# Fourier mixing with half of the cosines and sines: one stage of a two-network kernel, and where its instructions move

## The chip, the core and the metric

The program runs on one NeuronCore of a Trainium2 chip. The core has five engines with queues of their own that run side by side and wait for each other through semaphores: TensorE (PE, matrix products into PSUM), VectorE (DVE), ScalarE (ACT), GpSimd (POOL) and SyncE (SP, which issues most of the DMA transfers). The metric is the device time of one launch in microseconds (us); the kernel before takes 2376.23 us (median of three runs, 2372.3 to 2379.91).

## The reference

Two small networks run one after the other on 256 tokens of 1024 features, in float32. The last layer of the second network mixes its tokens by a Fourier transform instead of attention:

```python
def fourier_mix(h):
    b, l, d = h.shape
    hg = h.reshape(b, l, FNET_GROUPS, d // FNET_GROUPS).astype(F32)
    f = jnp.fft.fft2(hg, axes=(1, 3), norm="ortho").real
    return f.reshape(b, l, d).astype(h.dtype)
...
            y = fourier_mix(h) @ w_f
        x = x + g1 * rms_norm_2(y, norm_g[i, 1])
        h = modulate_2(rms_norm_2(x, norm_g[i, 2]), sh2, sc2)
        x = x + g2 * rms_norm_2(conv_ffn(h, ffn_w_up[i], ffn_conv_w[i], ffn_conv_b[i], ffn_w_down[i]), norm_g[i, 3])
```

With FNET_GROUPS = 4 and d = 1024, each of four groups is a block of 256 tokens by 256 features h, of which the real part of the two-dimensional transform is wanted. With C and S the 256 by 256 matrices of cosines and sines (divided by 16 here), the real part is C h C - S h S. Each row of C is symmetric about its middle (column 256-f equals column f) and each row of S antisymmetric, so that columns 0 to 128 of both determine the rest.

## The kernel before, in words

Everything is kept transposed: features lie on the 128 partitions and tokens along the free dimension, so a tile such as `hT` is eight chunks of 128 features by 256 tokens, two chunks to each Fourier group. The kernel is one straight program for each engine, written out by hand: `sp_program`, `pe_program`, `act_program`, `dve_program` and `pool_program` call small functions (`pe_fourier`, `dve_fourier`, ...) in the order in which the engine is to execute them, and each step waits for named counts of other engines. Nothing is reordered by a scheduler, so an instruction that waits holds up all that stands behind it on its engine.

PSUM banks 0 to 3 are given out in turn (`bank.turn`); a bank can be taken again when the instruction named in `bank.until` is done. Weights come in by DMA into ring slots of 1 MB. A matrix product with weights is made of three products of rounded halves (`mm3`): ACT copies a unit of 128x1024 weights to its high half (L386, `act_units`), and DVE or POOL subtracts that to get the low half (L392, `dve_units` and `pool_program`; the last argument of `sp_fm` says which of the two). Four buffers (HB) hold high halves, so at most four units are prepared ahead (`ahead`).

The Fourier stage of the last layer:

- The norm before it (tag `nA`) scales the eight chunks on DVE (L851) and shifts them on ACT (L816).
- `pe_fourier`, first step: for each group g and each half j of the tokens, two products of 128 tokens by 512 columns (256 cosines, 256 sines) into one bank, 16 products in all, begun when the norm is done with all eight chunks (`norm.done(7)`). DVE copies each bank to `fU` (L2767).
- Second step: for each group and each half i of the transformed features, four products of 128 by 256 that sum cosines with cosines and sines with negated sines, 32 in all. DVE copies each of the four banks to `fT` (L2770).
- ACT rounds each chunk to its high half (L867, `act_halves`), DVE forms the low half into `XL` (L872, `dve_halves`), and the output projection (`pe_out`, tag `out`) multiplies by `fourier_w_out`: 8 units of 24 products of 128x256.

Every matmul on float32 operands shows as two records in the trace, so 16 products are x32 there and 32 products x64; the products of rounded halves (fp32r, marked by an r at the tile's name) are one record each.

At the kernel's start there is one more place that matters here: `sp_mixer_first` loads the weights of the first projection ("qk", l, 0), whose low halves POOL forms, and `dve_program` runs the eight low halves of the first norm (`norm1[0].dve_low`, L858).

Of the kernel before, what the change touches and what calls it, by code (L numbers as in the profile page):

```python
# [16 lines left out]
T = 256  # L17
# [61 lines left out]
def dft_constants():  # L79
    n = np.arange(256)  # L80
    ang = 2.0 * np.pi * ((n[:, None] * n[None, :]) % 256) / 256.0
    cs = np.concatenate([np.cos(ang), np.sin(ang), -np.sin(ang)], axis=1) / 16.0
    return np.ascontiguousarray(cs.astype(np.float32))
# [140 lines left out]
def build(nc, A, out):  # L224
    CST_W = sum(w for _, w in CONST_COLS.values())
    with ExitStack() as ctx:
# [694 lines left out]
        def sp_mixer_first(sp, l):  # L921
            series()
            sp_fm(sp, ("qk", l, 0), A["w_in"][l], 0, "pool")
# [1633 lines left out]
        def act_out(act, l, hi, src, ready):  # L2557
            act_halves(act, ("out", l), hi, src, ready)
# [4 lines left out]
        def dve_out(dve, l, hi, src):  # L2563
            dve_halves(dve, ("out", l), hi, XL, src)
# [166 lines left out]
        fU = area(0)(4096)  # L2731
        fT = area(4096)(2048)
        fhi = area(6144)(2048, True)[1]

        def sp_fourier(sp):
            load(sp, ("dft",), by_rows(A["dft"]), 2, 768, MODS_IN)

        def pe_fourier(pe, norm):
            cs = chunk(("dft",), 2, 768)
            pe.wait_ge(*landed(("dft",)))  # L2740
            pe.wait_ge(*norm.done(7))
            for g in range(4):
                for j in range(2):
                    pe.wait_ge(*bank.turn("U", g, j))
                    for k in range(2):
                        t = mm(pe, bank["U", g, j][:, :], hT[:, (2 * g + k) * 256 + j * 128:(2 * g + k) * 256 + j * 128 + 128],
                               cs[:, k, 0:512], k == 0, k == 1)
                    t.then_inc(*pe_ffn.inc("U", g, j))
                    bank.until(("U", g, j), dve_ffn, "U", g, j)
            for g in range(4):  # L2750
                pe.wait_ge(*bank.turn("f", g))
# [7 lines left out]
                t.then_inc(*pe_ffn.inc("f", g))  # L2759
                bank.until(("f", g), dve_ffn, "f", g)  # L2760
            slots.until(("dft",), pe_ffn, "f", 3)
# [117 lines left out]
        def act_program(act):  # L2879
# [15 lines left out]
            act_out(act, 0, att.hi, att.oT, lambda k: dve_att["o", k])  # L2895
            for l in range(2):
                if l == 1:
                    normA[1].act(act)
                    act_units(act, ahead(("out", 1, 0, 0)))
                    act_out(act, 1, fhi, fT, lambda k: dve_ffn["f", k // 2])  # L2900
# [5 lines left out]
        def dve_program(dve):  # L2906
            dve_prologue(dve)
            for l in range(2):
                if l == 0:
# [5 lines left out]
                    for k in range(8):  # L2915
                        norm1[0].dve_low(dve, k)
# [8 lines left out]
            dve_out(dve, 0, att.hi, att.oT)  # L2925
            for l in range(2):
                if l == 1:
                    normA[1].dve(dve)
                    dve_units(dve, ahead(("out", 1, 0, 0)))
                    dve_fourier(dve)  # L2930
                    dve_out(dve, 1, fhi, fT)
# [86 lines left out]
```

## Time and profile before

| | |
|---|---|
| median of three runs | 2376.23 us (2372.3 to 2379.91) |
| profiled execution, its own time | 2380.68 us |
| its span in the trace | 2378.9 us |
| mean granted TensorE clock | 0.955 of full speed |
| PE busy | 2177.5 us (92%), 13659 records |
| DVE, ACT, POOL busy | 972.9, 671.7, 288.7 us |
| DMA | 657.92 MB, mean 277 GB/s |

The span is the time from the first to the last instruction of the profiled execution; 1.8 us lie outside it. A busy share is an average over stages with different limits, so the share of an engine says little on one stage; the chain of waits and the table of stretches say what the stage waits for. The granted clock has two levels, 2.4 GHz (1.00) and 1.2 GHz (0.50); a value between them is a mixture within the stretch. Busy times overlap: matmuls are pipelined, so the mean duration of one record is longer than the distance from one start to the next, and it is that distance (busy time over count) that adds up.

### The profile page before, as it was taken

The numbers are of one execution on the slowest core, as the hardware profiler recorded it, in microseconds if no ns is written. First come the engines' busy times: TensorE is split into PE (matmuls) and PEld (weight loads), VectorE is DVE, ScalarE is ACT, GpSimd is POOL, SyncE is SP. The second block draws the span as 40 slices with busy tenths as digits, with TensorE's granted clock in tenths as the row PEclk, the third lists the DMA queues.
The fourth block names the chain that finished last, engine by engine and source line by source line (L and its number), as shares of the span: only waits on it lengthen the run. The fifth ranks groups of instructions, "written<-read, shape, count | busy, mean of one in ns | idle before, by whom it ended". The sixth has DMA issues, their size and how long they took to land.

```text
span 2378.9 us, 31740 instructions
## 1 busy us (share of the span) xinstructions
PE 2177.5 (92%) x13659; PEld 1562.9 (66%) x13659; DVE 972.9 (41%) x1914; ACT 671.7 (28%) x1176; POOL 288.7 (12%) x147
## 2 busy tenths in 40 slices
PE   4998988999999999899899999999989899988998
PEld 3787674555555467777455555555756899968997
DVE  2465641111111146564221111111535677546776
ACT  2334421011111143443211011111123555424553
POOL 4543420000000034453000000000000000000000
PEclk7999989999999989999999999999999799887998
DMA  9865669999999976566899999996536365314550
GB/s 327 306 231 183 237 230 372 409 408 409 409 409 409 403 252 222 188 230 261 329 358 409 409 409 409 409 409 255 210 125 225 117 209 191 103 53 145 180 195 19
DMA packets 246844, 657.92 MB, mean 277 GB/s; under 512 B 12923, under 2 KB 124773, under 8 KB 234280
## 3 DMA queue, kind: packets, MB, share of 16 engines
q1 hardware_dynamic: 244032, 652.27, 72.6%
q8 instruction: 111, 1.82, 0.3%
q0 software_dynamic: 1184, 2.08, 0.3%
q10 hardware_dynamic: 1480, 1.45, 0.2%
q14 instruction: 37, 0.30, 0.0%
HBM read 654.70 MB, written 1.06 MB: 276 GB/s over the span
## 4 chain that ended last, share of the span: by engine, by line
PE 86%; DVE 9%; ACT 2%; SPq 1%; issue 1%; DMA 1%; ACTq 0%
PE ps L409 85%; DVE AR L1961 2%; SPq L341 1%; DVE AR L746 1%; DVE AR L2008 1%; DMA ring<-in_w_in 1%; DVE ARr L1636 0%; ACT HBr L386 0%; ACT AR L816 0%; PE ps L2462 0%; ACT AR L728 0%; DVE AR L2596 0%; DVE AR L1226 0%; DVE AR L1111 0%; DVE XLr L858 0%
## 5 line engine op out<-in xcount | busy, mean ns | idle before, releaser
L409 PE MATMUL ps<-ring,AR 128*64 128x512 f32 (+1 forms) x2016 | 522.9, 581 | 31.6 <-DVE AR L2008 31.6
L409 PE MATMUL ps<-XLr,HBr 128*128 128x256 f32 x1408 | 411.9, 293 | 44.8 <-DVE XLr L858 25.0
L409 PE MATMUL ps<-AR 128*128 128x128 f32 (+6 forms) x2088 | 380.8, 345 | 14.0 <-DVE AR L1942 7.5
L409 PEld LDWEIGHTS ps<-ring,AR 128*64 128x64 f32 (+1 forms) x2016 | 203.0, 141 | 271.4 <-issue 264.4
L392 POOL TENSOR_TENSOR ringr<-ring,HBr 128x1024 fp32r<-128x1024 f32 x112 | 270.9, 2434 | 803.2 <-ACT HBr L386 802.9
L409 PEld LDWEIGHTS ps<-AR 128*128 128x128 f32 (+2 forms) x2088 | 289.4, 191 | 119.8 <-issue 76.6
L409 PE MATMUL ps<-hTr,ringr 128*128 128x256 f32 x1280 | 367.4, 287 | 0.0
L409 PE MATMUL ps<-hTr,HBr 128*128 128x256 f32 x1280 | 367.0, 287 | 0.0
L386 ACT ACTIVATE HBr<-ring 128x1024 fp32r<-128x1024 f32 x260 | 266.1, 1050 | 238.0 <-PE ps L409 207.7
L409 PEld LDWEIGHTS ps<-XLr,HBr 128*128 128x128 f32 x1408 | 274.8, 195 | 66.0 <-issue 35.6
L409 PEld LDWEIGHTS ps<-hTr,ringr 128*128 128x128 f32 x1280 | 251.2, 196 | 0.8 <-issue 0.5
L409 PEld LDWEIGHTS ps<-hTr,HBr 128*128 128x128 f32 x1280 | 250.8, 196 | 0.0
L409 PE MATMUL ps<-ARr,HBr 128*128 128x256 f32 x1216 | 239.6, 284 | 2.6 <-DVE ARr L1636 2.6
L392 DVE TENSOR_TENSOR ringr<-ring,HBr 128x1024 fp32r<-128x1024 f32 x148 | 176.8, 1223 | 90.6 <-ACT HBr L386 90.6
L1992 DVE SCALAR_TENSOR_TENSOR AR<-AR,ps 128x512 f32<-128x512 f32 x32 | 22.0, 688 | 438.1 <-ACT AR L1987 438.1
L409 PEld LDWEIGHTS ps<-ARr,HBr 128*128 128x128 f32 x1216 | 195.4, 190 | 5.6 <-DVE ARr L1636 3.9
L409 PE MATMUL ps<-ARr,ringr 128*128 128x256 f32 x672 | 189.4, 282 | 0.0
L409 PE MATMUL ps<-HB,AR 128*64 128x512 f32 x464 | 154.6, 597 | 8.0 <-DVE AR L2008 8.0
L1987 ACT ACTIVATE AR<-ps 128x512 f32<-128x512 f32 x32 | 19.1, 598 | 418.8 <-PE ps L409 418.8
L409 PEld LDWEIGHTS ps<-ARr,ringr 128*128 128x128 f32 x672 | 127.6, 190 | 0.1
L2037 DVE COPY AR<-ps 128x512 f32<-128x512 f32 x32 | 22.1, 692 | 237.8 <-PE ps L409 237.8
L409 PE MATMUL ps<-XL,AR 128*64 128x512 f32 x240 | 108.1, 593 | 6.1 <-DVE AR L2008 3.2
(296 smaller groups left out, 2382.1 us busy)
## 6 DMA issues: line engine op xcount, KB each, us to landing
ring<-in_w_expert_in SPq DMA_DIRECT2D x155, 1024.0 KB, 14.9
ring<-in_w_expert_out SPq DMA_DIRECT2D x81, 1024.0 KB, 10.9
ring<-in_mod_w SPq DMA_DIRECT2D x48, 1024.0 KB, 6.6
ring<-in_ffn_w_up SPq DMA_DIRECT2D x44, 1024.0 KB, 5.2
ring<-in_w_in SPq DMA_DIRECT2D x40, 1024.0 KB, 5.4
ring<-in_w_ada SPq DMA_DIRECT2D x40, 1024.0 KB, 7.1
HB<-in_w_expert_in SPq DMA_DIRECT2D x35, 1024.0 KB, 14.8
HB<-in_w_expert_out SPq DMA_DIRECT2D x23, 1024.0 KB, 12.1
```

The source lines that it names most:

```text
L341: sp.op.dma_start(dst, src).then_inc(*slot_in[s].inc(*name))
L386: act.op.activation(hi, raw, ACT.Copy).then_inc(*act_hi.inc(*name))
L392: lane.op.tensor_tensor(lo, sel(chunk(of, k, w)), hi.bitcast(F32), ALU.subtract).then_inc(*count.inc(*name))
L409: return pe.op.matmul(out_, lhsT, rhs, start=start, stop=stop, **kw)
L746: dve.op.reciprocal(rs[:, 0:n], rs[:, 0:n]).then_inc(*dve_norm.inc(tag, "rstd"))
L1961: dve.op.tensor_scalar(m.x["x", l, p][:, k * 128:(k + 1) * 128], bank["xg", l, p, 1][:, c], m.coef[:, k:k + 1], m.shift[:, k:k + 1], ALU.m ...
L1987: act.op.activation(m.th["th", l, p], bank["up", l, p, 0][:, :], ACT.Tanh, scale=0.5).then_inc(*act_moe.inc("th", l, p))
L1992: dve.op.scalar_tensor_tensor(t, t, 1.0, bank["up", l, p, 0][:, :], ALU.add, ALU.mult).then_inc(*dve_moe.inc("gated", l, p))
L2008: dve.op.tensor_copy(m.h["h", l, p], bank["turn", l, p][:, :]).then_inc(*dve_moe.inc("turn", l, p))
L2037: dve.op.tensor_copy(m.y["y", l, p][:, 512:1024], bank["down", l, p, 1][:, :]).then_inc(*dve_moe.inc("y", l, p))
```

## The change

Three things are edited.

1. The table of the transform holds columns 0 to 128 of the cosines and of the sines (2 x 129 = 258 columns in place of 768). The first step makes products of 258 columns, and it begins a group when that group's two chunks of the norm are there. ACT, not DVE, copies each bank to `fU`, and DVE makes a reversed copy `fR` of columns 1 to 128, which stands for the mirrored features. The second step makes products of 129 columns, with cosines and sines in two halves of a bank: from `fU` for the features 0 to 127 (i = 0) and from `fR` for the others (i = 1). ACT copies the sines' half to `fS`; DVE forms the tokens 0 to 128 as sum or difference of the two halves, and the tokens 255 to 129 as the other of the two, written backwards.
2. The work between the steps is interleaved: one weight unit is prepared for each group (ACT and DVE), and the high and the low half of a chunk are formed right behind the next chunk's sums.
3. In the first network, layer 0, the low halves of the first two weight units move from POOL to DVE: one ahead of the eight low halves of the norm, one in their middle.

```diff
 def dft_constants():
-    n = np.arange(256)
-    ang = 2.0 * np.pi * ((n[:, None] * n[None, :]) % 256) / 256.0
-    cs = np.concatenate([np.cos(ang), np.sin(ang), -np.sin(ang)], axis=1) / 16.0
+    n, f = np.arange(256), np.arange(129)
+    ang = 2.0 * np.pi * ((n[:, None] * f[None, :]) % 256) / 256.0
+    sin = np.where(f % 128 == 0, 0.0, np.sin(ang))
...
         def sp_mixer_first(sp, l):
-            sp_fm(sp, ("qk", l, 0), A["w_in"][l], 0, "pool")
+            sp_fm(sp, ("qk", l, 0), A["w_in"][l], 0, "dve" if l == 0 else "pool")
...
-            pe.wait_ge(*norm.done(7))
             for g in range(4):
+                pe.wait_ge(*norm.done(2 * g + 1))
                 for j in range(2):
                     pe.wait_ge(*bank.turn("U", g, j))
                     for k in range(2):
-                        t = mm(pe, bank["U", g, j][:, :], hT[:, (2 * g + k) * 256 + j * 128:(2 * g + k) * 256 + j * 128 + 128],
-                               cs[:, k, 0:512], k == 0, k == 1)
+                        t = mm(pe, bank["U", g, j][:, 0:2 * NF], hT[:, (2 * g + k) * 256 + j * 128:(2 * g + k) * 256 + j * 128 + 128],
+                               cs[:, k, :], k == 0, k == 1)
                     t.then_inc(*pe_ffn.inc("U", g, j))
-                    bank.until(("U", g, j), dve_ffn, "U", g, j)
+                    bank.until(("U", g, j), act_ffn, "U", g, j)
             for g in range(4):
-                pe.wait_ge(*bank.turn("f", g))
                 for i in range(2):
-                    for n in range(4):
-                        j, isin = n // 2, n % 2
-                        pe.wait_ge(*dve_ffn["U", g, j])
-                        a = (2 * g + j) * 512 + isin * 256 + i * 128
-                        t = mm(pe, bank["f", g][:, sl(i)], fU[:, a:a + 128], cs[:, j, 512:768] if isin else cs[:, j, 0:256],
-                               n == 0, n == 3)
+                    pe.wait_ge(*bank.turn("f", g, i))
+                    for sine in range(2):
+                        for j in range(2):
+                            pe.wait_ge(*(dve_ffn["R", g, j] if i else act_ffn["U", g, j]))
+                            n = 2 * g + j
+                            a = (2 * n + sine) * 128 if i else (2 * n + sine) * NF
+                            t = mm(pe, bank["f", g, i][:, sl(sine, NF)], (fR if i else fU)[:, a:a + 128], cs[:, j, sl(sine, NF)],
+                                   j == 0, j == 1)
+                    t.then_inc(*pe_ffn.inc("f", g, i))
+                    bank.until(("f", g, i), dve_ffn, "f", g, i)
...
+        def act_fourier(act):
+            for g in range(4):
+                for j in range(2):
+                    act.wait_ge(*pe_ffn["U", g, j])
+                    act.op.activation(fU[:, sl(2 * g + j, 2 * NF)], bank["U", g, j][:, 0:2 * NF], ACT.Copy).then_inc(*act_ffn.inc("U", g, j))
+                act_units(act, place.get(("out", 1, 0, 0), 0) + g + 1)
+            for k in range(9):
+                if k < 8:
+                    g, i = k // 2, k % 2
+                    act.wait_ge(*fS.turn(g, i))
+                    act.wait_ge(*pe_ffn["f", g, i])
+                    act.op.activation(fS[g, i], bank["f", g, i][:, NF:2 * NF], ACT.Copy).then_inc(*act_ffn.inc("sines", g, i))
+                    fS.until((g, i), dve_ffn, "f", g, i)
+                if k:
+                    act_half(act, ("out", 1), fhi, fT, dve_ffn["f", (k - 1) // 2, (k - 1) % 2], k - 1)
         def dve_fourier(dve):
             for g in range(4):
                 for j in range(2):
-                    dve.wait_ge(*pe_ffn["U", g, j])
-                    dve.op.tensor_copy(fU[:, (2 * g + j) * 512:(2 * g + j + 1) * 512], bank["U", g, j][:, :]).then_inc(*dve_ffn.inc("U", g, j))
+                    n = 2 * g + j
+                    dve.wait_ge(*act_ffn["U", g, j])
+                    dve.op.tensor_copy(v3(fR[:, sl(n)], 2), v3(fU[:, sl(n, 2 * NF)], 2)[:, :, T // 2:0:-1]).then_inc(*dve_ffn.inc("R", g, j))
+                dve_units(dve, place.get(("out", 1, 0, 0), 0) + g + 1)
             for g in range(4):
-                dve.wait_ge(*pe_ffn["f", g])
-                dve.op.tensor_copy(fT[:, sl(g, 512)], bank["f", g][:, :]).then_inc(*dve_ffn.inc("f", g))
+                for i in range(2):
+                    dve.wait_ge(*act_ffn["sines", g, i])
+                    f, c, s = fT[:, sl(2 * g + i)], bank["f", g, i][:, 0:NF], fS[g, i]
+                    near, far = (ALU.add, ALU.subtract) if i else (ALU.subtract, ALU.add)
+                    dve.op.tensor_tensor(f[:, 0:NF], c, s, near).then_inc(*dve_ffn.inc())
+                    dve.op.tensor_tensor(f[:, T - 1:T // 2:-1], c[:, 1:T // 2], s[:, 1:T // 2], far).then_inc(*dve_ffn.inc("f", g, i))
+                    if g + i:
+                        k = 2 * g + i - 1
+                        dve_half(dve, ("out", 1), fhi, XL, fT, k)
+            dve_half(dve, ("out", 1), fhi, XL, fT, 7)
...
                     for k in range(8):
+                        if k % 4 == 0:
+                            dve_units(dve, k // 4 + 1)
                         norm1[0].dve_low(dve, k)
```

`act_half` and `dve_half` are one turn of `act_halves` and `dve_halves`. In the two programs the preparation of four units at once, which stood between the norm and the Fourier stage, is gone.

On VectorE, in the Fourier stage, the kernel before has these rows. The scaling of the norm (`hT<-xT,ps`) comes first, then four weight units, the copies out of PSUM, all low halves (`XLr`), and the units of the projection.

```order
L851 TENSOR_TENSOR hT<-xT,ps 128x256 x8
L392 TENSOR_TENSOR ringr<-ring,HBr 128x8x128 x4
L2767 COPY AR<-ps 128x512 x8
L2770 COPY AR<-ps 128x512 x4
L872 TENSOR_TENSOR XLr<-AR,ARr 128x256 x8
```

In the changed kernel the same stretch of VectorE has more rows. Behind the scaling stand four pairs like the first two rows here (this is the fourth: two reversed copies and a unit), then the sums begin; each further chunk has two sums and a low half as the last three rows.

```order
L2787 COPY AR<-AR 128x256 x2
L393 TENSOR_TENSOR ringr<-ring,HBr 128x8x128
L2794 TENSOR_TENSOR AR<-ps,AR 128x129
L2795 TENSOR_TENSOR AR<-ps,AR 128x127
L2794 TENSOR_TENSOR AR<-ps,AR 128x129
L2795 TENSOR_TENSOR AR<-ps,AR 128x127
L1637 TENSOR_TENSOR XLr<-AR,ARr 128x256
```

Twelve copies of 512 elements out of PSUM are replaced by eight reversed copies of 256 within SBUF and sixteen sums of 129 or 127; each low half now stands right behind the sums of the next chunk, where before it stood behind all copies.

On VectorE at the kernel's start, around the coefficient of the first norm (`smal<-mods,cols`) and up to the first evacuation of the mixer (L1527), the kernel before has this (lines carry other numbers after the change: L392 is L393, L858 is L859).

```order
L718 COPY modrow<-ps 128x512
L708 TENSOR_TENSOR mods<-ps,cols 128x16
L839 SCALAR_TENSOR_TENSOR smal<-mods,cols 128x8
L858 TENSOR_TENSOR XLr<-biasB,hTr 128x256 x8
L1527 TENSOR_SCALAR AR<-ps 128x512
```

And in the changed kernel:

```order
L840 SCALAR_TENSOR_TENSOR smal<-mods,cols 128x8
L393 TENSOR_TENSOR ringr<-ring,HBr 128x8x128
L859 TENSOR_TENSOR XLr<-biasB,hTr 128x256 x4
L393 TENSOR_TENSOR ringr<-ring,HBr 128x8x128
L859 TENSOR_TENSOR XLr<-biasB,hTr 128x256 x4
L1528 TENSOR_SCALAR AR<-ps 128x512
```

Two weight units have come in, the second between the fourth and the fifth low half of the norm; on GpSimd the first two of its units are gone.

## Rows read from the trace of the kernel before

**Rows 1.** The chain of waits, 2080 to 2145 us: start us, us, what.

```profile
2084.18 4.05 ACT hT L816 x8
...
2088.36 30.76 PE ps L409 x96
...
2120.31 22.87 PE ps L409 x192
```

**Rows 2.** Stretches: from:to us, length, busy us (records) per engine, PEclk, DMA, GB/s.

```profile
1800.00:1850.00 50.00, 46.77 (x324) 34.65 (x316) 24.17 (x52) 18.40 (x35) 0.00 (x0) 0.97 0.57 190
...
2088.00:2094.00 6.00, 5.64 (x7) 2.52 (x8) 4.80 (x5) 4.01 (x5) 0.00 (x0) 0.50 0.02 3
...
2120.00:2143.00 23.00, 22.69 (x192) 22.68 (x192) 11.09 (x15) 8.01 (x9) 0.00 (x0) 1.00 0.35 113
...
2200.00:2250.00 50.00, 50.00 (x421) 50.00 (x420) 38.83 (x61) 28.11 (x42) 0.00 (x0) 1.00 0.58 196
```

**Rows 3.** Groups by shape, PE, 2088 to 2121 us: busy us, mean ns, idle before.

```profile
L409 PE MATMUL ps<-ring,hT 128*128 128x512 f32 x32 | 16.9, 695 | 4.7 <-ACT hT L816 4.7
L409 PE MATMUL ps<-ring,AR 128*128 128x256 f32 x64 | 14.0, 379 | 0.0
```

**Rows 4.** Timeline of weight loads in the first step: start us, us, what.

```profile
2093.62 0.34 PEld L409 LDWEIGHTS ps<-ring,hT 128*128 128x128 f32 x1 [0.52 <-issue]
2094.40 0.19 PEld L409 LDWEIGHTS ps<-ring,hT 128*128 128x128 f32 x1 [0.45 <-issue]
```

**Rows 5.** Timeline of PE at the last layer's feed-forward start.

```profile
2167.61 0.55 PE L409 MATMUL ps<-XLr,HBr 128*128 128x256 f32 x1 [2.55 <-DVE XLr L858]
...
2172.70 0.34 PE L409 MATMUL ps<-hTr,ringr 128*128 128x256 f32 x1
```

**Rows 6.** Two stretches that hold only 128x1 products on float32.

```profile
15.20:19.10 3.90, 3.85 (x34) 3.76 (x32) 0.81 (x2) 2.77 (x7) 0.00 (x0) 0.99 1.01 422
2074.00:2082.00 8.00, 6.99 (x32) 6.90 (x32) 4.84 (x15) 3.40 (x9) 0.00 (x0) 0.50 1.10 349
```

**Rows 7.** Timeline of PE: 128x128 products on float32.

```profile
84.74 2.05 PE L409 MATMUL ps<-cst,AR 128*128 128x128 f32 x16
```

**Rows 8.** Groups by shape, ACT: first two of the whole span, then 2080 to 2124 us.

```profile
L1928 ACT ACTIVATE AR<-ps,mods,smal 128x128 f32<-128x128 f32 x128 | 48.2, 457 | 159.6 <-PE ps L409 159.6
...
L1932 ACT ACTIVATE AR<-ps 128x256 f32<-128x256 f32 x32 | 12.3, 385 | 17.3 <-PE ps L1919 17.3
...
L386 ACT ACTIVATE HBr<-ring 128x1024 fp32r<-128x1024 f32 x5 | 4.9, 1043 | 2.9 <-PE ps L409 2.9
...
L867 ACT ACTIVATE ARr<-AR 128x256 fp32r<-128x256 f32 x8 | 2.9, 408 | 25.7 <-DVE AR L2770 25.7
```

**Rows 9.** Groups by shape, DVE: first two of the whole span, then 2080 to 2124 us.

```profile
L1171 DVE TENSOR_TENSOR AR<-ps,cst 128x128 f32<-128x128 f32 x16 | 4.5, 282 | 4.0 <-PE ps L409 4.0
...
L627 DVE COPY crep<-smal 128x256 f32<-128x256 f32 x1 | 0.3, 293 | 0.0
...
L392 DVE TENSOR_TENSOR ringr<-ring,HBr 128x1024 fp32r<-128x1024 f32 x4 | 4.6, 1220 | 2.8 <-ACT HBr L386 2.8
...
L872 DVE TENSOR_TENSOR XLr<-AR,ARr 128x256 fp32r<-128x256 f32 x8 | 2.8, 416 | 0.0
```

**Rows 10.** Timeline at the start of the program, one engine after another.

```profile
46.28 2.00 ACT L386 ACTIVATE HBr<-ring 128x1024 fp32r<-128x1024 f32 x2 [8.20 <-DMA ring<-in_w_in]
...
49.60 0.45 DVE L858 TENSOR_TENSOR XLr<-biasB,hTr 128x256 fp32r<-128x256 f32 x1 [17.09 <-ACT hTr L825]
50.40 3.62 DVE L858 TENSOR_TENSOR XLr<-biasB,hTr 128x256 fp32r<-128x256 f32 x5 [0.35 <-ACT hTr L825]
...
47.41 4.86 POOL L392 TENSOR_TENSOR ringr<-ring,HBr 128x1024 fp32r<-128x1024 f32 x2 [0.93 <-ACT HBr L386]
...
52.60 0.58 PE L409 MATMUL ps<-XLr,HBr 128*128 128x256 f32 x1 [1.43 <-DVE XLr L858]
```

**Rows 11.** The instructions of L858, 48 to 58 us: duration ns min/median/max.

```profile
L858 DVE TENSOR_TENSOR XLr<-biasB,hTr x8: 412/420/2148, 49.6 to 54.7; 128x256 fp32r<-128x256 f32 x8
```

More of the change, by code:

```diff
@@ L79, in dft_constants @@
 def dft_constants():
-    n = np.arange(256)
-    ang = 2.0 * np.pi * ((n[:, None] * n[None, :]) % 256) / 256.0
-    cs = np.concatenate([np.cos(ang), np.sin(ang), -np.sin(ang)], axis=1) / 16.0
-    return np.ascontiguousarray(cs.astype(np.float32))
+    n, f = np.arange(256), np.arange(129)
+    ang = 2.0 * np.pi * ((n[:, None] * f[None, :]) % 256) / 256.0
+    sin = np.where(f % 128 == 0, 0.0, np.sin(ang))
+    return np.ascontiguousarray((np.concatenate([np.cos(ang), sin], axis=1) / 16.0).astype(np.float32))
 def bucket_onehot():
@@ L2555, in pe_out, with act_out @@
                 pe_fm(pe, ("out", l, g), hi, XL, halves_done(("out", l)), (dve_norm, ("pA", l), "scaled", 2 * g + 1))
-        def act_out(act, l, hi, src, ready):
-            act_halves(act, ("out", l), hi, src, ready)
+        def act_out(act, l):
             for g in range(4):
@@ L2561, in act_out, with dve_out @@
                     act_units(act, ahead(("out", l, g, m), 1))
-        def dve_out(dve, l, hi, src):
-            dve_halves(dve, ("out", l), hi, XL, src)
+        def dve_out(dve, l):
             for g in range(4):
@@ L2728, in dve_ffn_all @@
                         dve_units(dve, ahead(("dn", l, g - 1, i), 1))
-        fU = area(0)(4096)
-        fT = area(4096)(2048)
-        fhi = area(6144)(2048, True)[1]
+        NF = T // 2 + 1
+        take_f = area(0)
+        fU, fR, fT = take_f(16 * NF), take_f(16 * 128), take_f(2048)
+        fhi = take_f(2048, True)[1]
+        fS = in_turn([take_f(NF) for _ in range(4)])
         def sp_fourier(sp):
-            load(sp, ("dft",), by_rows(A["dft"]), 2, 768, MODS_IN)
+            load(sp, ("dft",), by_rows(A["dft"]), 2, 2 * NF, MODS_IN)
         def pe_fourier(pe, norm):
-            cs = chunk(("dft",), 2, 768)
+            cs = chunk(("dft",), 2, 2 * NF)
             pe.wait_ge(*landed(("dft",)))
-            pe.wait_ge(*norm.done(7))
             for g in range(4):
+                pe.wait_ge(*norm.done(2 * g + 1))
                 for j in range(2):
@@ L2759, in pe_fourier @@
-                t.then_inc(*pe_ffn.inc("f", g))
-                bank.until(("f", g), dve_ffn, "f", g)
-            slots.until(("dft",), pe_ffn, "f", 3)
+                    pe.wait_ge(*bank.turn("f", g, i))
[6 more added lines that the diff above has]
+                                   j == 0, j == 1)
@@ new lines, in pe_fourier @@
+                    t.then_inc(*pe_ffn.inc("f", g, i))
+                    bank.until(("f", g, i), dve_ffn, "f", g, i)
+            slots.until(("dft",), pe_ffn, "f", 3, 1)
+        def act_fourier(act):
[13 more added lines that the diff above has]
+                    act_half(act, ("out", 1), fhi, fT, dve_ffn["f", (k - 1) // 2, (k - 1) % 2], k - 1)
@@ L2894, in act_program @@
             act_attend(act, att)
-            act_out(act, 0, att.hi, att.oT, lambda k: dve_att["o", k])
+            act_halves(act, ("out", 0), att.hi, att.oT, lambda k: dve_att["o", k])
+            act_out(act, 0)
             for l in range(2):
@@ L2898, in act_program @@
                     normA[1].act(act)
-                    act_units(act, ahead(("out", 1, 0, 0)))
-                    act_out(act, 1, fhi, fT, lambda k: dve_ffn["f", k // 2])
+                    act_fourier(act)
+                    act_out(act, 1)
                 postA[l].act(act)
@@ L2924, in dve_program @@
             dve_attend(dve, att)
-            dve_out(dve, 0, att.hi, att.oT)
+            dve_halves(dve, ("out", 0), att.hi, XL, att.oT)
+            dve_out(dve, 0)
             for l in range(2):
@@ L2928, in dve_program @@
                     normA[1].dve(dve)
-                    dve_units(dve, ahead(("out", 1, 0, 0)))
                     dve_fourier(dve)
-                    dve_out(dve, 1, fhi, fT)
+                    dve_out(dve, 1)
                 else:
```

## The prediction, made before the changed kernel was run

> **What bounds the kernel now.** The views were read in this order: the page's busy shares (PE 92%), the chain of waits, the stretches around the Fourier stage, the groups by shape there, then the timeline of each engine at the two places that the change touches.
>
> In the Fourier stage the chain of waits is TensorE alone: ACT shifts the eight chunks of the norm until 2088.2 us, then one unbroken piece of 96 records takes 30.76 us, one copy on DVE and one low half follow, and the output projection starts at 2120.31 [rows 1]. The stretches say the same: its two groups of products fill those 30.9 us, with no wait inside [rows 3]. So what PE does less here is gained one for one, as long as the two other engines keep up. From the projection on PE stays the bound: 192 records in 22.87 us, and in the feed-forward layer PE is busy 50.00 of 50 us [rows 1, 2]. A projection that starts earlier ends earlier by as much.
>
> One thing is special to the stage: PE comes from a pause and runs at the lower level (1.2 GHz, granted 0.50) at first. The weight loads take 0.34 us up to 2093.62 and 0.19 us from 2094.40, so the level rose about 5.6 us after the start at 2088.36 [rows 2, 4]. At the next start, 2167.61, it rose at 2172.7, after 5.1 us [rows 5].
>
> **The change part by part.** All times are on the clock of the profiled execution.
>
> Start. Group 0 needs chunks 0 and 1 only. ACT's eight shifts take 4.05 us, 0.51 each, so chunk 1 is there at 2084.18 + 1.01 = 2085.19; with the 0.14 us that PE took after the last chunk before, it starts at 2085.33 in place of 2088.36: 3.0 us gained. At the lower level a group costs PE 3.5 us and ACT needs 1.0 us to shift two chunks, so no later group waits for the norm. The bounds are 0 (if the earlier start is spent wholly at the lower level) and 3.0; I take 3.0, since the level rose after about as much work time at both starts seen.
>
> First step. 32 records of 512 columns took from 2088.36 to 2105.1, 16.8 us. Now they have 258 columns. The nearest row is 64 records of 256 columns in 14.0 us at the upper level, 0.218 each [rows 3], so 32 x 0.218 = 7.0 us at full speed. With 5.8 us at the lower level half of that time is lost, 2.9 us: 9.9 us, ending at 2095.2. Gained 6.9 us. With 5.1 or 7 us at the lower level it is 9.5 or 10.5 us; with the lower level throughout it is 14.0.
>
> Second step. 64 records of 256 columns, 14.0 us, become 64 of 129. They do not fall to half. In the trace 32 records with a single column still take 3.85 us at the upper level, 0.120 each, and 6.99 us, 0.218 each, at the lower [rows 6]: there the weight load of 128 columns sets the pace. 16 records of 128 columns took 2.05 us, 0.128 each [rows 7]. I take 0.125: 8.0 us, ending at 2103.2. Gained 6.0 us. Bounds: 64 x 0.120 = 7.7 and, if nothing is gained by the narrower product, 14.0.
>
> The Trainium skill, in "TensorE: Matmul & The Clock Gate", section LDWEIGHTS, has a load take as long as its columns at 1.2 GHz, whatever the product behind it; for 128 columns that is 107 ns and would make the second step 6.8 us, 1.2 us less. The rows have 120 ns for a load with next to nothing behind it, and the measurement decides.
>
> Handover. Before, the last product ended at 2119.1 and PE waited for a copy, a high and a low half until 2120.31: 1.2 us. Now the low half of chunk 0 is made while PE is still in the second step, so that the projection begins at once: 1.2 us gained.
>
> Whether ACT and DVE keep up, from their rows [rows 8, 9]. ACT: a bank of 258 columns 0.39 us, a weight unit 1.04, so 1.8 us for a group; it starts at 2088.2, when the norm is done, and its last unit ends at about 2096.6. DVE: two reversed copies 0.3 each (row of 256 elements within SBUF: 0.29; if the reversed reading costs double, 0.42) and a unit 1.22: 1.9 us for a group, last unit at about 2098.1. PE's banks: U of group 2 takes the bank that ACT emptied at 2088.6, and PE needs it at 2092. In the second step DVE has for each of eight halves two sums (0.21 apart, 0.28 alone) and a low half (0.35 in a row, 0.42 alone): 0.8 to 1.0 us; ACT a copy of 129 (0.3 to 0.46) and a high half 0.41: 0.7 to 0.9 us; PE 1.0 us. Sums 0 end at 2098.6, sums 7 at 2098.6 + 7 x 0.8 = 2104.2, low half 7 at 2105.0; with 1.0 us for each, at 2106.6. PE, in the projection since 2103.2 at 0.357 us a chunk, comes to chunk 7 at 2105.7. So the wait is 0 to 0.9 us, and PE's four banks cost nothing (sums 0 free the bank that product group 4 wants at 2099.2). I take 0.5 us lost for all the handings over.
>
> Moved weight units. Four units in place of four are made by ACT and DVE before the projection; the transfers are old (issued before 2071), and the rest of SP's queue is unchanged but for a smaller table.
>
> The program's start. POOL's first two units go to DVE. They bound nothing: PE's first product waits for the norm's first low half, begun at 49.60, and ACT came to the norm only at 48.2 because it first had to make units whose weights landed at 46.28 [rows 10]. So nothing is gained by units 0 and 1 being early. Unit 0 falls into the 17.09 us for which DVE waits ahead of 49.60 [rows 10]. Unit 1, 1.22 us, now stands ahead of low half 4. DVE was held in the low half of chunk 1 for 2.15 us while POOL worked on units 2 and 3, which ends at 52.3 in both kernels [rows 10, 11]. Behind it DVE makes low halves 2 and 3 (52.6 to 53.4), unit 1 (to 54.7) and low half 4 (to 55.1); PE, which starts chunk 1 at 52.60 and needs some 0.7 us a chunk at the lower level (twice the 0.357 of the projection), wants chunk 4 at 54.7. 0.4 us lost, 0.3 counted. Bounds: 0 and 2.0 (if unit 1 is stretched as that low half was).
>
> Sum: 3.0 + 6.9 + 6.0 + 1.2 - 0.5 - 0.3 = 16.3 us. The profiled execution took 2380.68 us, 4.45 above the median of its kernel; less 16.3 it would be 2364.4. Taken from the median, 2376.23 - 16.3 = **2359.9, forecast 2360 us**.
>
> **The rivals.**
>
> 1. ACT and DVE pace the second step. If each half goes through its chain without overlap, it costs a copy 0.46, two sums 0.56, a high half 0.41, a low half 0.42 and four handings over of 0.04: 2.0 us, eight times 16 us from 2096.6. Low half 7 comes at 2112.6, the projection's first unit ends 6.9 us late. Gain 16.3 + 0.5 - 6.9 = 9.9: 2366 us. For it: the two engines hand each chunk over four times. Against: ACT's queue has the sines of chunk k+1 ahead of the high half of k, so that the work overlaps.
>
> 2. The lower level lasts through both steps. 14.0 + 64 x 0.218 = 28.0 us, the projection starts at 2113.3: gain 7.0 - 0.8 = 6.2, 2370 us. Against: pauses of this size do not bring the level down in the attention stage, where PE is busy 46.8 of 50 us at 0.97 [rows 2].
>
> 3. The slower side: the lower level goes on into the projection, because PE, with short products and a wait at each of the sixteen banks, is no longer kept full. Loads took 6.99 us at the lower level for 3.85 at the upper, a factor of 1.82 [rows 6], and the projection's 22.87 us would become 41.5 [rows 1]: 18.7 more. 7.0 - 0.8 - 18.7 = -12.5: 2388.7 us. It decides when the lower level lasts beyond 2091.1 by more than 2 x 16.3 = 33 us, to about 2124. The Trainium skill speaks for rivals 2 and 3: "TensorE: Matmul & The Clock Gate", section on psum-queue depth-cycling, says that small idle times between groups of products, while PE cycles through banks, make the clock fall back and rise again.
>
> 4. The gain is given back or isn't there: later work waits for weights, or something unseen in the rest of the program moves by as much. Against: PE is full in the feed-forward layer with DMA at 0.58 [rows 2]. 2376 us.
>
> **How the numbers follow.** Forecast 0.80, rival 1 0.08, rival 2 0.05, rival 3 0.03, rival 4 0.04. The median itself moved by 3.8 us either way in three runs; the sizes add 2 us down (a shorter lower level, a second step at 7.7, no waits) and 4 us up (waits 1.3, start 2.0, second step at 0.14): 2354 to 2367 us, which takes in rival 1. A measurement of this kernel can tell about 0.3%, 7.1 us, from no change. Faster by more than that: nearly all of the forecast (0.78), 0.07 of rival 1 and 0.02 of rival 2, 0.87. Within it: 0.09. Slower: rival 3 and a little of rival 4, 0.04.
>
> **What would show it.** The first 258-column product 1.1 us after ACT's first shift; loads at 0.34 us until about 2091 and 0.19 after; the first step in 10 us and the second in 8; less than 0.5 us idle on PE ahead of the projection, and the projection still 22.9 us; ahead of it DVE steps of 0.8 to 1.0 us a half; at the start of the program PE's fifth chunk delayed by under 0.5 us. The forecast is wrong if 129-column records stand more than 0.14 us apart, if PE waits for ACT or DVE by over 2 us in the stage, or if granted 0.50 lasts past 2095.

## The result, and the profile after

The changed kernel takes 2358.19 us (median of four runs, 2352.08 to 2360.78) against 2375.66 us, a ratio of 0.9916 with a 95% interval of 0.9895 to 0.9936. Two further comparisons of the same kernel, in five rounds each, gave 0.9921 (0.9909 to 0.9934) and 0.9921 (0.9904 to 0.9938). The forecast was 2360, with 2354 to 2367 as its range. The gain of the medians is 17.5 us, and the last two intervals leave room for 15 to 23. So the total alone can't test a forecast gain of 16.3 us closely; its terms can.

The profiled execution took 2355.85 us. The page's first lines, with busy us, share of the span and records of PE:

```profile
span 2354.1 us, 31772 instructions
...
PE 2160.1 (92%) x13659; PEld 1555.8 (66%) x13659; DVE 975.6 (41%) x1928; ACT 675.9 (29%) x1192; POOL 284.6 (12%) x145
```

PE lost 17.4 us of busy time and kept its share: it bounds the kernel as before. The chain of waits over the Fourier stage (start us, us, what):

```profile
2077.33 1.10 ACT hT L817 x2
...
2078.57 39.62 PE ps L410 x288
```

Before, the chain went through all eight of ACT's shifts, 96 records of PE, a copy and a low half, and then 192 records [rows 1]. Now it leaves ACT after the second shift and PE does the two steps and the whole projection in one piece. The timeline of PE names the pieces:

```profile
2078.57 9.85 PE L410 MATMUL ps<-ring,hT 128*128 128x258 f32 x32 [1.79 <-ACT hT L817]
2088.25 7.31 PE L410 MATMUL ps<-ring,AR 128*128 128x129 f32 x64
2095.32 0.36 PE L410 MATMUL ps<-XLr,HBr 128*128 128x256 f32 x1
```

and the stretches between these starts (length, busy us and records of PE, PEld, DVE, ACT, POOL, then PEclk, DMA, GB/s):

```profile
2078.57:2088.25 9.68, 9.68 (x32) 7.97 (x33) 5.10 (x12) 7.94 (x16) 0.00 (x0) 0.72 0.01 2
2088.25:2095.32 7.07, 7.07 (x66) 7.07 (x64) 6.87 (x22) 5.10 (x16) 0.00 (x0) 1.00 0.00 0
2095.32:2118.18 22.86, 22.85 (x195) 22.64 (x193) 10.40 (x14) 8.48 (x11) 0.00 (x0) 1.00 0.35 115
```

The stage, counted here and below from ACT's first shift to the first product of the projection, lasts 2095.32 - 2077.33 = 17.99 us; before it was 2120.31 - 2084.18 = 36.13 [rows 1]. That is 18.1 us. The first step went from 16.8 to 9.68 us with a granted clock of 0.72, the second from 14.0 [rows 3] to 7.07. The weight-load column of the second step points to what limits it: PEld is busy for 7.07 of 7.07 us. (It is also nearly full in the projection, so this alone proves nothing; the products with 65 columns below do.) The projection itself is unchanged (22.87, now 22.86).

DVE and ACT in the second step, where both run steadily, and DVE's last low half (start us, us; the bracket is idle time before, and its releaser):

```profile
2093.00 0.28 DVE L2794 TENSOR_TENSOR AR<-ps,AR 128x129 f32<-128x129 f32 x1
2093.20 0.28 DVE L2795 TENSOR_TENSOR AR<-ps,AR 128x127 f32<-128x127 f32 x1
2093.39 0.41 DVE L1637 TENSOR_TENSOR XLr<-AR,ARr 128x256 fp32r<-128x256 f32 x1
2093.73 0.28 DVE L2794 TENSOR_TENSOR AR<-ps,AR 128x129 f32<-128x129 f32 x1
...
2096.88 0.42 DVE L1637 TENSOR_TENSOR XLr<-AR,ARr 128x256 fp32r<-128x256 f32 x1 [0.15 <-ACT ARr L1522]
```

```profile
2094.24 0.42 ACT L1522 ACTIVATE ARr<-AR 128x256 fp32r<-128x256 f32 x1
2094.70 0.28 ACT L2777 ACTIVATE AR<-ps 128x129 f32<-128x129 f32 x1
2094.97 0.42 ACT L1522 ACTIVATE ARr<-AR 128x256 fp32r<-128x256 f32 x1
```

A half costs DVE 0.73 us (2093.00 to 2093.73), less than PE's 0.88 (7.07 over eight). The last low half ends at 2097.3, while PE, in the projection since 2095.32, comes to that chunk 2.5 us after its start, at 2097.9. From its first product of the stage on, PE waits for nothing.

The trace of after comes to the stage 6.9 us earlier than that of before (2077.33 against 2084.18), and 18.1 + 6.9 is the whole difference of the two spans, 24.8, to 0.2. The median of the runs shows only 17.5. What the 6.9 us are was the first question for the experiments.

### The profile page after: what moved, and what is told of

It reads as the page before. It is cut to its first block, busy times and chain, and to the rows that moved or that the text cites. A ratio compares the mean times of both kernels' runs of the same rounds, so it can differ in the third digit from the quotient of the medians.

```text
span 2354.1 us, 31772 instructions
## 1 busy us (share of the span) xinstructions
PE 2160.1 (92%) x13659; PEld 1555.8 (66%) x13659; DVE 975.6 (41%) x1928; ACT 675.9 (29%) x1192; POOL 284.6 (12%) x145
## 3 DMA queue, kind: packets, MB, share of 16 engines
q8 instruction: 111, 1.82, 0.3%
## 4 chain that ended last, share of the span: by engine, by line
PE 86%; DVE 9%; ACT 3%; SPq 1%; issue 1%; DMA 1%; ACTq 0%; DVEq 0%
PE ps L410 85%; DVE AR L1962 2%; DVE AR L747 1%; DVE AR L2009 1%; SPq L342 1%; DMA ring<-in_w_in 1%; ACT AR L817 0%; ACT HBr L387 0%; DVE ARr L1637 0%; PE ps L2463 0%; ACT hTr L826 0%; ACT AR L729 0%; DVE AR L2595 0%; DVE AR L1227 0%; DVE AR L1112 0%
## 5 line engine op out<-in xcount | busy, mean ns | idle before, releaser
L410 PE MATMUL ps<-ring,AR 128*64 128x512 f32 (+2 forms) x2016 | 516.3, 578 | 31.5 <-DVE AR L2009 31.5
L410 PEld LDWEIGHTS ps<-ring,AR 128*64 128x64 f32 (+1 forms) x2016 | 198.0, 141 | 269.4 <-issue 263.9
L393 POOL TENSOR_TENSOR ringr<-ring,HBr 128x1024 fp32r<-128x1024 f32 x110 | 266.8, 2440 | 800.3 <-ACT HBr L387 800.3
L393 DVE TENSOR_TENSOR ringr<-ring,HBr 128x1024 fp32r<-128x1024 f32 x150 | 179.5, 1223 | 94.0 <-ACT HBr L387 93.7
```

The lines of the kernel that those rows point to most:

```text
L393: lane.op.tensor_tensor(lo, sel(chunk(of, k, w)), hi.bitcast(F32), ALU.subtract).then_inc(*count.inc(*name))
L410: return pe.op.matmul(out_, lhsT, rhs, start=start, stop=stop, **kw)
```

## The experiments

**The kernel before, once more.** No edit.

> The kernel before once more, for a second trace of it. The changed kernel's trace came to the Fourier stage 6.9 us earlier than the trace of before (ACT's first shift of the norm at 2077.33 against 2084.18 us). Theory A: most of this is chance in the transfers of the first layers; then this trace's shift differs from 2084.18 by 1 to 7 us too, and its stage, from the shift to the start of the output projection, is again 36.1 us within 0.2. Theory B: it is the moved weight units; then this trace comes to the stage at 2084 within 1 us.

The timeline has:

```profile
2081.58 16.91 PE L409 MATMUL ps<-ring,hT 128*128 128x512 f32 x32 [4.74 <-ACT hT L816]
2098.32 13.98 PE L409 MATMUL ps<-ring,AR 128*128 128x256 f32 x64
2113.51 0.36 PE L409 MATMUL ps<-XLr,HBr 128*128 128x256 f32 x1 [1.21 <-DVE XLr L872]
```

and the chain of the same trace the shift:

```profile
2077.40 4.05 ACT hT L816 x8
```

The stage is 36.11 us again, but it begins at 2077.40: 6.8 us earlier than in the first trace of the same kernel. So two traces of one program differ by that much ahead of the stage, and theory A holds in that the 6.9 us are chance. That the chance lies in the transfers is not shown. The trace with the earlier stage had the weights of its third and fourth unit later (46.96 us against 46.28), and its first projection still began 0.7 us later (50.86 against 50.20). At 100 us into the program it is 0.4 us behind the first trace, instruction for instruction, and at 420 us it is 5.9 us ahead. Two stretches of PE there, in the first trace and then in this one (the third figure from the end is the granted clock):

```profile
100.00:115.00 15.00, 13.04 (x93) 9.93 (x93) 5.84 (x10) 3.48 (x4) 5.34 (x4) 0.89 0.92 341
280.00:350.00 70.00, 60.90 (x450) 55.01 (x451) 32.00 (x82) 20.59 (x41) 21.75 (x9) 0.85 0.66 249
```

```profile
100.00:115.00 15.00, 13.05 (x106) 10.76 (x105) 6.21 (x10) 4.47 (x4) 6.83 (x4) 1.00 0.92 354
280.00:350.00 70.00, 60.88 (x468) 54.07 (x469) 32.61 (x84) 19.96 (x40) 21.32 (x9) 0.91 0.62 236
```

The first trace has the lower granted clock in both, and it does fewer records in the same time. Whether the clock is the cause or follows from waits is not shown. Over all traces taken here the first shift stands between 2075.0 and 2085.1 us, with the moved units and without.

**The whole change, the Fourier stage alone, the moved units alone.** In the same rounds. For the second, the changed kernel with

```diff
-            sp_fm(sp, ("qk", l, 0), A["w_in"][l], 0, "dve" if l == 0 else "pool")
+            sp_fm(sp, ("qk", l, 0), A["w_in"][l], 0, "pool")
...
-                        if k % 4 == 0:
-                            dve_units(dve, k // 4 + 1)
```

and for the third the kernel before with the same lines the other way round.

> The changed kernel once more, timed beside its parts. Theory A (the gain is the Fourier stage, 18.1 us): 0.9920 to 0.9930 of the time of before. Theory B (stage and moved units, 25 us): 0.9895. In the trace the stage lasts 18.0 us within 0.3 under both.

> The changed Fourier stage alone; the first two weight units' low halves stay on POOL and DVE's eight low halves stay in a row. Theory A: as fast as the whole change or 1 us faster, ratio to before 0.992; the stretch from PE's first chunk to its last product of the first projection 9.5 to 10 us. Theory B: 7 us slower than the whole change, ratio 0.9925 where the whole has 0.9895.

> The moved weight units alone, with the old Fourier stage. Theory A: no change, 0 to 1 us slower, ratio 1.000; DVE makes unit 1 between low halves 3 and 4 and PE waits less than 0.4 us for it. Theory B: 7 us faster, ratio 0.997.

| | median us | ratio to before, 95% interval | stage us | first projection us |
|---|---|---|---|---|
| whole change | 2357.94 | 0.9921 (0.9909 to 0.9934) | 17.97 | 10.28 |
| Fourier stage alone | 2358.15 | 0.9922 (0.9909 to 0.9935) | 17.91 | 9.75 |
| moved units alone | 2376.01 | 1.0005 (0.9995 to 1.0015) | 36.09 | 9.57 |
| before (17 runs) | 2375.72 | | 36.1 | 9.42 and 9.73 |

The stage in the whole change comes from these two pieces of the chain, less the projection's 22.86 us: 2081.07 + 39.59 - 22.86 - 2079.83 = 17.97.

```profile
2079.83 1.10 ACT hT L817 x2
2081.07 39.59 PE ps L410 x288
```

All of the gain is in the Fourier stage, and the moved units are worth nothing that can be measured. The last column is the stretch from PE's first product of the first network to the end of its first two units: 9.6 to 10.9 us in the five traces with moved units that I read there, 9.4 to 9.75 in the three without. Inside, PE does wait for the low half behind unit 1, somewhat less than was forecast. In the trace of after, DVE makes unit 1 between the low halves:

```profile
50.64 1.21 DVE L393 TENSOR_TENSOR ringr<-ring,HBr 128x1024 fp32r<-128x1024 f32 x1
51.78 1.41 DVE L859 TENSOR_TENSOR XLr<-biasB,hTr 128x256 fp32r<-128x256 f32 x4
```

```profile
51.55 0.41 PE L410 MATMUL ps<-XLr,HBr 128*128 128x256 f32 x1
...
52.24 0.58 PE L410 MATMUL ps<-XLr,HBr 128*128 128x256 f32 x1
...
53.05 0.41 PE L410 MATMUL ps<-XLr,HBr 128*128 128x256 f32 x1
```

At the lower level a chunk takes 0.64 us, so chunk 4, the fifth, begins at 52.24 in place of 52.19, 0.05 us late. But it then takes 0.81 itself, with a first record of 0.58, like the one at 50.10 in this trace, which stands behind 1.42 us of waiting. Chunk 5 is 0.22 us late, where 0.4 was forecast. The other traces with moved units that were read here show the same 0.80 or 0.81 us for this chunk, and those without show 0.64. The longer stretch of that trace (10.86 us) has another reason: PE began 2.5 us earlier than in the first trace of before (47.70 against 50.20), yet records became short between 56.3 and 56.6 in both, so that more was done at the lower level. What sets that moment isn't shown here.

The next five kernels were each executed once, for their traces. Their times, 2353.89 to 2361.61 us, hold the chance ahead of the stage and rank nothing (the fastest is one whose stage is longer), so only the stage is read.

**No start by groups.**

```diff
-                pe.wait_ge(*norm.done(2 * g + 1))
+                pe.wait_ge(*norm.done(7))
```

> The changed kernel, but the first step waits for all eight chunks of the norm as before. Theory A (the earlier start is worth itself): the stage, from ACT's first shift to the projection's start, is 18.0 + 3.0 = 21.0 us. Theory C (part of the early work is done at the lower clock level, whose end is set by something other than the start of this step): 19.5 to 20 us, since the early 3 us do only half of their work, and the first step then lasts less than 9.7 us.

```profile
2080.59 4.05 ACT hT L817 x8
...
2084.78 39.89 PE ps L410 x288
```

2084.78 + 39.89 - 22.86 - 2080.59 = 21.22 us, 3.2 more. Theory A holds, theory C falls: the time at the lower level moved with the start of the step (the first step took 9.95 us, not less than 9.7), so the start is worth all of its 3 us.

**High and low halves behind the sums.**

```diff
             for k in range(9):
...
-                if k:
-                    act_half(act, ("out", 1), fhi, fT, dve_ffn["f", (k - 1) // 2, (k - 1) % 2], k - 1)
+            for k in range(8):
+                act_half(act, ("out", 1), fhi, fT, dve_ffn["f", k // 2, k % 2], k)
...
-                    if g + i:
-                        k = 2 * g + i - 1
-                        dve_half(dve, ("out", 1), fhi, XL, fT, k)
-            dve_half(dve, ("out", 1), fhi, XL, fT, 7)
+            for k in range(8):
+                dve_half(dve, ("out", 1), fhi, XL, fT, k)
```

> The changed kernel, but all high and low halves are made behind the last sums, as the old stage did. Theory A: the projection waits about 1.2 to 1.6 us for the first low half, stage 19.3 us, and then is paced by DVE's low halves at 0.35 us, which PE's 0.357 a chunk hides. Rival: DVE, freed of low halves between the sums, is done with them 2.5 us earlier, so that the wait is under 0.5 us.

```profile
2075.49 1.10 ACT hT L817 x2
2076.73 17.05 PE ps L410 x96
...
2095.13 22.86 PE ps L410 x192
```

The stage is 19.64 us, 1.7 more than with the interleaving, and the chain breaks between the second step and the projection again, where PE waits 1.37 us. This is the handover of before (1.2 us), and its rival (DVE done early enough) is out. The 1.7 us are this wait and about 0.3 us of the last record, which overlaps the next product where there is no wait.

**Four units at once, ahead of the Fourier stage.**

```diff
-                act_units(act, place.get(("out", 1, 0, 0), 0) + g + 1)
...
-                dve_units(dve, place.get(("out", 1, 0, 0), 0) + g + 1)
...
                     normA[1].act(act)
+                    act_units(act, ahead(("out", 1, 0, 0)))
                     act_fourier(act)
```

and the same on DVE.

> The changed kernel, but ACT and DVE prepare all four weight units between the norm and the Fourier stage, as before, instead of one for each group. Theory A (the new order matters little, since PE has four banks): ACT empties the first bank at about 4.9 us after the last shift of the norm instead of at once; PE, at the lower level, has filled four banks by then, so it waits 0 to 1 us; DVE's reversed copies and sums come in time; stage 18.0 to 19.0 us. Rival (interleaving is needed): PE waits for ACT's copies at each bank, stage over 20 us.

```profile
2081.63 6.40 PE L410 MATMUL ps<-ring,hT 128*128 128x258 f32 x16 [1.79 <-ACT hT L817]
2088.63 3.72 PE L410 MATMUL ps<-ring,hT 128*128 128x258 f32 x16 [0.60 <-ACT AR L2770]
2092.19 7.31 PE L410 MATMUL ps<-ring,AR 128*128 128x129 f32 x64
2099.26 0.36 PE L410 MATMUL ps<-XLr,HBr 128*128 128x256 f32 x1
```

From the shift at 2080.39 the stage is 18.87 us, 0.9 more. PE fills four banks and then waits 0.60 us for ACT. The four banks hide most of the four units, as theory A had it.

**The second step with products of 256 columns, and with 65.** The first edit leaves the values used as they are (ACT's copy of the sines then reads the bank's elements 383 to 511, not shown here); the second leaves out 64 of the 129 columns.

```diff
-                            t = mm(pe, bank["f", g, i][:, sl(sine, NF)], (fR if i else fU)[:, a:a + 128], cs[:, j, sl(sine, NF)],
+                            t = mm(pe, bank["f", g, i][:, sl(sine)], (fR if i else fU)[:, a:a + 128], cs[:, j, 2 * sine:2 * sine + 256],
```

```diff
-                            t = mm(pe, bank["f", g, i][:, sl(sine, NF)], (fR if i else fU)[:, a:a + 128], cs[:, j, sl(sine, NF)],
+                            t = mm(pe, bank["f", g, i][:, sine * NF:sine * NF + 65], (fR if i else fU)[:, a:a + 128], cs[:, j, sine * NF:sine * NF + 65],
```

> The changed kernel with products of 256 columns in the second step instead of 129 (the same numbers are used of them). Theory A: 64 records at 0.218, 14.0 us, stage 25 us: the narrower product is worth 6.9 us. Rival: the second step is paced by ACT and DVE, and then it lasts about 9 us, since their work is unchanged.

> The changed kernel with 65 of the 129 columns in each product of the second step; the other 64 are left out. Theory A (the weight load of 128 columns sets the pace): 64 records still take 7.0 us, 0.110 each. Rival (the columns set it, 129 of them at four passes being 0.108 a record too): 3.6 to 4 us. If loads alone needed the 0.120 that the one-column products showed, it would be 7.7 us.

The wide one:

```profile
2086.02 13.97 PE L410 MATMUL ps<-ring,AR 128*128 128x256 f32 x64
2099.65 0.47 PE L410 MATMUL ps<-XLr,HBr 128*128 128x256 f32 x1
```

and the narrow one, with its stretch of the second step:

```profile
2088.65 7.25 PE L410 MATMUL ps<-ring,AR 128*128 128x65 f32 x64
```

```profile
2088.65:2095.71 7.06, 7.06 (x66) 7.06 (x64) 6.87 (x22) 5.09 (x16) 0.00 (x0) 1.00 0.00 0
```

With 256 columns the stage lasts from the shift at 2075.04 to 2099.65, 24.61 us, 6.6 more; the step itself takes 13.63, 0.213 a record. With 65 it is 2095.71 - 2077.73 = 17.98, as with 129. Halving the columns once was worth 6.6 us, halving them again nothing, so the columns alone don't set the pace at 129. An equal time alone would also fit a pace set by ACT and DVE, whose work is the same in all three. They are ruled out by their own rows: PE is busy for 7.06 of 7.06 us with no wait for either, and DVE needs 0.73 us for a half where PE needs 0.88. What is left is the load of 128 weights, with PEld busy for 7.06 of 7.06 us.

**Spare products in TensorE's pauses.** To price the lower clock level, the changed kernel with products of constants into the bank that the next real product overwrites:

```diff
+        WARM = {"pA": (3, 2), "pF": (3, 2), "ffn": (4, 2), "nA": (4, 2)}
+        def warm(pe, b, n):
+            pe.wait_ge(*q_cst["all"])
+            for _ in range(n):
+                mm(pe, b[:, 0:256], C("ones"), C("cos"), True, True)
...
+                    if (g, j) == (0, 0):
+                        warm(pe, bank["U", 0, 0], 3)
```

The pairs are the numbers ahead of a norm's means and ahead of its spread; five more stand ahead of each feed-forward layer (not shown here).

> The changed kernel with spare products of 256 columns (float32, constants by constants, into the bank that the next real product overwrites) in TensorE's pauses around the norms of the second network's layers: 3 or 4 ahead of the means, 2 ahead of the spread, 3 ahead of the Fourier step, 5 ahead of the feed-forward layer. Theory L (the lower clock level after each pause costs PE half of the first 5 us): the level stays up or rises before the real products, first Fourier step 7.0 instead of 9.7 us, stage 15.3 instead of 18.0 us, and some 2 to 3 us less at each of the two feed-forward starts and 1 us at each norm's means; in all 8 to 14 us less than the changed kernel, ratio to before 0.987. Rival M: the spare products run at the lower level and only delay the real ones, 0.4 us each too many; 0 to 10 us slower than the changed kernel.

```profile
2082.77 1.75 PE L410 MATMUL ps<-cst 128*128 128x256 f32 x6
2084.68 7.24 PE L410 MATMUL ps<-ring,hT 128*128 128x258 f32 x32 [0.16 <-ACT hT L827]
2091.76 7.46 PE L410 MATMUL ps<-ring,AR 128*128 128x129 f32 x64
2098.98 0.36 PE L410 MATMUL ps<-XLr,HBr 128*128 128x256 f32 x1
```

With the shift at 2083.54 the stage is 15.44 us, 2.5 less: the first step takes 7.08 us at a granted 1.00 in place of 9.68 at 0.72. So for the stage theory L holds. For the whole it doesn't: 2356.97 us, 0.9914 (0.9898 to 0.9931), which can't be told from the changed kernel. Three stretches of this trace show where the spare products help and where they don't:

```profile
2064.31:2069.09 4.78, 4.78 (x40) 4.62 (x39) 0.00 (x0) 3.35 (x5) 0.00 (x0) 1.00 0.67 231
...
2073.94:2076.64 2.70, 2.32 (x18) 1.98 (x16) 2.70 (x9) 1.67 (x4) 0.00 (x0) 0.98 1.10 348
2076.64:2080.07 3.43, 3.43 (x16) 3.43 (x17) 1.29 (x4) 1.17 (x3) 0.00 (x0) 0.50 1.09 354
```

The level stayed up through the first spare products and the means behind them, and these means took 3.5 us in place of 5.1. The next four spare products took 2.63 us at a granted 0.66; the means behind them had the upper level for their first half and the lower for the second (6.1 us, 7.0 in the changed kernel). Both gains are small, and in the layer before there is a loss (rival M):

```profile
1856.87 3.78 PE L410 MATMUL ps<-cst 128*128 128x256 f32 x8 [1.43 <-DVE AR L2605]
1860.44 6.82 PE L410 MATMUL ps<-cst,AR 128*128 128x1 f32 x32
```

Four spare products took 3.57 us there, at a granted 0.50, where PE had a pause of 2.3 us in the changed kernel; the means begin 6.0 us behind the spread in place of 3.5. The losses over the whole span were not added up.

**More spare products, between the one-column ones.** Added: one product of 128 columns behind each of the first seven chunks of the means, in a further bank.

> As the kernel with spare products, with one more spare product of 128 columns behind each of the first seven pairs of one-column products in the means. In its trace without them the level was 1.00 while the spare products and the first means ran and fell again behind a stretch that held only one-column products. Theory L2 (one-column products do not keep the level up): now the means ahead of the Fourier stage take 5.5 to 6 us instead of 6.3 (7.0 in the changed kernel), the first Fourier step stays at 7.1 us, and the whole is 3 to 6 us faster than the changed kernel in the same call, ratio to before 0.990. Rival: the spare products delay the real ones by as much as the level gives; the same time as the changed kernel.

> The changed kernel on the same chip and in the same rounds, for the comparison: ratio to before 0.992, the stage from ACT's first shift to the projection 18.0 us.

It came out against both: 2368.15 us, 0.9966 (0.9953 to 0.9979), 9 us slower than the changed kernel in the same rounds (2359.07, 0.9921 with 0.9904 to 0.9938). Ahead of the Fourier stage it did what was hoped (means in 5.2 us, first step 7.08). But the norms behind the projection and the feed-forward layer have their squares ready early, and there PE is itself what the means wait for:

```profile
2067.12 0.50 PE L410 MATMUL ps<-cst,AR 128*128 128x1 f32 x4
2067.48 0.47 PE L410 MATMUL ps<-cst 128*128 128x128 f32 x2
...
2071.16 0.86 PE L410 MATMUL ps<-cst,AR 128*128 128x1 f32 x4
2071.88 0.78 PE L410 MATMUL ps<-cst 128*128 128x128 f32 x2
```

Each chunk costs 0.67 us with a spare product, and 0.45 without (3.63 over eight), and the level fell at 2071 all the same. These means took 6.0 us, against 5.1 in the changed kernel. That this makes up the 9 us was not worked out. A version with spare products only ahead of the Fourier step, where they took 2.6 us off the first step, is the obvious one; it was not run.

## Why the prediction was right, point by point

- *Start, 3.0 us.* Measured by undoing it: 3.2; between the traces of before and after 2.9 (4.18 us from the first shift to the first product, then 1.24, where 1.15 was forecast).
- *First step, 9.9 us with 5.8 at the lower level.* 9.68, and 7.08 with the level up: 2.6 us lost to the level, 2.9 forecast.
- *Second step, 8.0 us.* 7.07. The mechanism was right (the weight load, not the columns) and the size was off: 0.110 a record, not 0.125. The rows gave 3.85 us for 32 and 2.05 for 16 [rows 6, 7]. But a busy time over a short group holds more than the pace: the tail of its last record (about 0.27 us, the whole length of one of them) and a slower start. (The stretch of rows 6 also counts 34 records on PE; 32 of them are the one-column products.) Read from start to start, both groups have the pace of 0.110 already: in the first the 4th record starts at 15.67 and the 32nd at 18.79, in the second the 2nd at 84.96 and the 16th at 86.52. So the trace of before held the right number, and it was divided wrongly. For the same reason the 256-column record is 0.213 (13.63 us in the wide run), not 0.218, and the lower level costs a factor of 2.0 on loads (0.218 over 0.110) and not the 1.82 of rival 3. The Trainium skill ("TensorE: Matmul & The Clock Gate", section LDWEIGHTS) gives a load as its columns over 1.2 GHz, by which a load of 128 columns is estimated at 107 ns. That was nearer than my reading of the rows; the measured pace is 3 to 4 ns above it.
- *Handover, 1.2 us.* 1.2 in the traces of before; 1.7 by undoing the interleaving in the changed kernel.
- *Waits for ACT and DVE, 0.5 us lost.* None. DVE needed 0.73 us a half, below the 0.8 to 1.0 worked out. Rival 1 is out: PE has no wait inside the step, and the last low half was done 0.6 us before PE came to it.
- *The start of the program, 0.3 us lost.* 0.2 in the trace, and a ratio of 1.0005 (0.9995 to 1.0015) for the units alone. The mechanism was the forecast one: low half 4 stands behind unit 1, and PE comes to its chunk just before it is done.
- *Rivals 2 and 3* (the lower level lasts) are out: granted 1.00 in the second step and in the projection. The Trainium skill's section on psum-queue depth-cycling ("TensorE: Matmul & The Clock Gate"), which spoke for them, has small idle times between groups of products as its condition. That condition was not met: PE took its four banks in turn, sixteen times in all, without a pause, so the stage neither bears the section out nor refutes it. With one pause of 0.60 us, in the run with four units at once, the granted clock behind it was 1.00. *Rival 4* is out too: the span lost what the stage lost.

The stage gave 18.1 us where 16.6 were forecast (16.3 with the program's start); the error is the second step (0.9), the waits (0.5) and the first step (0.2), less 0.1 at the start. That the median came within 2 us of the forecast is in part luck, since it moved by less than the stage (17.5 us) and single executions differ by several us ahead of the stage; the terms are the better test, and they hold.

## What to carry to other kernels

Where the chain through a stage is one unbroken piece of one engine, the sum of that engine's records is the forecast, and everything else is only a check that it stays unbroken. Halving the moving columns pays until the load of the stationary columns is as long as the product, here near 130 columns on float32 (0.213 us a record at 256 columns, 0.110 at 129 and at 65). Beyond that one would need fewer products, not narrower ones, which no run here tried. Take the pace of a record from start to start, not from a busy time over a short group. And when two traces differ by more than the medians do, take a second trace of the same kernel before explaining the difference.

## What was not expected

- The same one-column products met both levels: in the trace of before they ran at a granted 0.50 ahead of the stage, with PE busy for 6.99 of 8.00 us, and at 0.99 at the start of the program [rows 6]. With spare products ahead of them the level was 1.00 in one norm's means and fell to 0.50 within the next. Products of 128 columns between them kept it up once (from 2078.6 on) and not another time (2071). What decides it stays open.
- Reading and writing in reverse cost nothing: a reversed copy of 256 elements within SBUF took 0.29 us, like a copy of as many from single repeated elements [rows 9] (no plain forward copy of that size within SBUF is in the trace of before), and a sum of 127 written backwards 0.28, like the 129 written forwards.
- Where this program differs from run to run, it is ahead of the stage. ACT could begin the third and fourth unit between 43.5 and 47.6 us (traces without spare products), which alone does not order the traces, and its first shift in the Fourier layer stood within 10 us (2075.0 to 2085.1), while the stage itself repeated to 0.1 us.
